# Last token tile of a decoder step: block loads and a VectorE transpose in place of TensorE transposes

## The reference, cut to what matters

```
hp = concatenate([meta, x_prompt], axis=1)      # 16 + 1024 rows of 1024
hs = x_sample                                   # 8 rows of 1024
# layer, for hp and hs alike
hn = rmsnorm(h, norm_mix)
z  = hn @ w_in                                  # 1024 -> 3584
u_in, c_gate, b_gate, q, k, v, g = split(z)
y_conv = b_gate * causal_conv3(c_gate * u_in)
o = retention(rotary(q), rotary(k) * QK_DIM**-0.5, v)   # 4 heads, chunks of 128
y_ret = head_rmsnorm(o) * silu(g)
h = h + concatenate([y_conv, y_ret]) @ w_out
h = h + square(relu(rmsnorm(h, norm_mlp) @ w_up)) @ w_down
```

## Time and profile before

| | us |
|---|---|
| median of 3 runs (1128.28 to 1129.99) | 1129.04 |
| the profiled execution | 1128.74 |
| its span | 1126.9 |
| PE busy | 1114.5 (99%) |
| VectorE busy | 784.3 (70%) |
| GpSimd busy | 551.5 (49%) |
| ScalarE busy | 418.1 (37%) |

### The profile page before, as it was taken

The page is one execution under the profiler, slowest core; times in us unless marked ns, Lnnn a source line. Parts: engine busy times, 40 slices in busy tenths (PEclk is TensorE's granted clock), DMA queues, the critical chain, the costliest instruction groups (busy, mean ns, idle before and its releaser), DMA issues.

```text
span 1126.9 us, 21879 instructions
## 1 busy us (share of the span) xinstructions
PE 1114.5 (99%) x8339; PEld 1096.2 (97%) x8339; DVE 784.3 (70%) x1171; ACT 418.1 (37%) x861; POOL 551.5 (49%) x535
## 2 busy tenths in 40 slices
PE   9999999999999999999999999999999999999996
PEld 7799999999999999999999999999999999999996
DVE  5455656566466766788777777777877776877856
ACT  6422313123124333543333333335552543444414
POOL 0154253252240611143322423223999899999992
PEclk9999999999999999999999999999999999999999
DMA  8951341422321231255344353438962544464314
GB/s 223 235 140 49 98 122 48 130 75 77 94 76 59 77 113 64 69 188 180 122 151 150 124 173 127 151 114 277 341 198 68 163 151 149 134 189 151 95 38 152
DMA packets 187482, 150.37 MB, mean 133 GB/s; under 512 B 32989, under 2 KB 149957, under 8 KB 187391
## 3 DMA queue, kind: packets, MB, share of 16 engines
q1 hardware_dynamic: 182295, 145.93, 41.4%
q10 hardware_dynamic: 5096, 3.20, 0.9%
HBM read 104.92 MB, written 44.20 MB: 132 GB/s over the span
## 4 chain that ended last, share of the span: by engine, by line
PE 98%; DMA 1%; SPq 1%; DVE 0%; issue 0%; DVEq 0%; ACT 0%
PE pair L2045 19%; PE pair L2046 19%; PE pair L2047 19%; PE pair L1832 8%; PE pair L1834 8%; PE pair L1833 8%; PE pair L2022 3%; PE pair L2024 3%; PE pair L2023 3%; PE pair L1890 1%; PE pair L1891 1%; PE pair L1893 1%; PE pair L1940 1%; PE pair L1943 1%; PE pair L1950 1%; PE pair L1939 1%
## 5 line engine op out<-in xcount | busy, mean ns | idle before, releaser
L2045 PE MATMUL pair<-m_hi,dn_hi 128*128 128x258 f32 (+2 forms) x896 | 254.7, 284 | 0.2 <-issue 0.2
L2046 PE MATMUL pair<-b_lo,up_hi 128*128 128x258 f32 x896 | 253.6, 283 | 0.0
L2045 PE MATMUL pair<-b_hi,up_hi 128*128 128x258 f32 x896 | 253.6, 283 | 0.0
L2046 PE MATMUL pair<-m_lo,dn_hi 128*128 128x258 f32 (+2 forms) x896 | 253.6, 283 | 0.0
L2047 PE MATMUL pair<-m_hi,dn_lo 128*128 128x258 f32 (+2 forms) x896 | 253.3, 283 | 0.0
L2047 PE MATMUL pair<-b_hi,up_lo 128*128 128x258 f32 x896 | 252.2, 282 | 0.0
L1832 PE MATMUL pair<-x_hi,w_both 128*128 128x344 f32 (+2 forms) x576 | 188.7, 328 | 0.1
L1834 PE MATMUL pair<-x_hi,w_both 128*128 128x344 f32 (+2 forms) x576 | 184.5, 320 | 0.0
L1833 PE MATMUL pair<-x_lo,w_both 128*128 128x344 f32 (+2 forms) x576 | 184.2, 320 | 0.0
L1800 DVE TENSOR_TENSOR hid<-pair,hid 128x516 f32<-128x516 f32 (+2 forms) x194 | 124.6, 642 | 75.1 <-PE pair L2047 72.1
L2045 PEld LDWEIGHTS pair<-b_hi,up_hi 128*128 128x128 f32 x896 | 169.3, 189 | 1.0 <-issue 0.8
(11 more groups left out here) (224 smaller groups left out, 2037.8 us busy)
## 6 DMA issues: line engine op xcount, KB each, us to landing
m_raw<-m_dram SPq DMA_DIRECT2D x56, 516.0 KB, 5.0
m_dram<-hid SPq DMA_DIRECT2D x64, 258.0 KB, 3.7
up_raw<-w_up_dram SPq DMA_DIRECT2D x32, 512.0 KB, 4.9
dn_raw<-w_down_dram SPq DMA_DIRECT2D x128, 128.0 KB, 2.4
w_raw<-w_in_dram SPq DMA_DIRECT2D x27, 512.0 KB, 3.7
m_dram<-hid SPq DMA_DIRECT2D x16, 774.0 KB, 3.8
h_dram<-hid SPq DMA_DIRECT2D x8, 516.0 KB, 3.1
h_in<-h_dram SPq DMA_DIRECT2D x16, 258.0 KB, 5.5
```

Of the source, the lines that this page charges most:

```text
L2045: m_.matmul(to, shs[k], mhs[k], start=STARTS[i] and k == 0, stop=False, skip_group_check=more)
L2046: m_.matmul(to, shs[k], mls[k], start=False, stop=False, skip_group_check=more)
```

## The change

Tile 8 is turned like tiles 2 to 7. `load_end_blocks` loads its rows a second time in runs of 32 floats into buffer 0 of `x_blk` with eight DMAs, four of 16 partitions (meta) and four of 8 (samples), once tile 6 has been turned out of that buffer. They stand on SyncE's queue behind tile 8's row loads and ahead of the tables. `x_turn(8)` waits for the eight loads and turns them into a new tile `x_last` with one transpose of 256 elements a partition. ScalarE's copies and VectorE's subtractions for tile 8 read `x_last` in place of PSUM and take all eight groups at once. PE's eight transposes of tile 8 go. The counts that later code waits for grow by one turn and eight loads.

```diff
-TURN0 = len(BLK)
-MOVED0 = 64 * len(BLK) // 2
+TURN0 = len(BLK) + 1
+MOVED_B = 64 * len(BLK) // 2
+MOVED_A = MOVED_B + 128
...
+        x_last = at("x_last", [KT, SQ], F32, o + XT * CH * 4 + 4 * KT * 56)
...
+            def load_end_blocks():
+
+                sp.wait_ge(turned, XT - 1 - BLK[2] + 1)
+                for src, r0, r1 in ((meta, 0, META), (xs.rearrange("b s d -> (b s) d"), META, LAST)):
+                    rows = src.rearrange("b (k q a) -> q b k a", q=4, a=SQ)
+                    for q in range(4):
+                        sp.dma_start(x_blk[0][SQ * q + r0:SQ * q + r1, :, 0, :], rows[q]).then_inc(sq_moved, 16)
...
+            load_end_blocks()
             sp.dma_start(cosr[:, :], io["cos_t"]).then_inc(tab_in, 16)
...
+                if i == XT - 1:
+                    act.wait_ge(turned, TURN0)
+                    s.activation(x_end[:, :, 0:LAST], x_last[:, :, 0:LAST], ACT.Copy)
+                    s.activation(x_end[:, :, LAST:32], x_last[:, :, 0:32 - LAST], ACT.Copy)
+                    for c0, c1, r0 in ENDS:
+                        ins = s.activation(x_hi[:, :, c0:c1], x_last[:, :, r0:r0 + c1 - c0], ACT.Copy)
+                    ins.then_inc(xhi_done, 2)
+                    return
...
+                if i == XT - 1:
+                    dve.wait_ge(xhi_done, 2 * i + 2)
+                    d.tensor_tensor(x_end[:, :, 32:32 + LAST], x_last[:, :, 0:LAST], x_end[:, :, 0:LAST], ALU.subtract).then_inc(pack_ready, 2)
+                    for c0, c1, r0 in ENDS:
+                        ins = d.tensor_tensor(x_lo[:, :, c0:c1], x_last[:, :, r0:r0 + c1 - c0], x_hi[:, :, c0:c1], ALU.subtract)
+                    ins.then_inc(xlo_done, 2)
+                    return
...
+                if i == XT - 1:
+                    dve.wait_ge(sq_moved, MOVED_A)
+                    d.transpose(x_last[:, :, :], x_blk[0][:, :, 0, :]).then_inc(turned, 1)
+                    return
...
-                if i + 1 in BLK:
+                if i + 1 in BLK or i + 1 == XT - 1:
                     x_turn(i + 1)
...
             for i in range(XT):
                 v_rows(i)
-                if i + 2 < XT and i + 2 not in BLK:
-                    transposes(i + 2)
```

More of the change, by code:

```diff
@@ L528, in turn_rest @@
             def turn_rest(h):
-                sp.wait_ge(sq_moved, MOVED0 + 176 * h + 16)
+                sp.wait_ge(sq_moved, MOVED_A + 176 * h + 16)
                 sp.dma_start(k_meta[0:META, :].rearrange("r (b s) -> r b s", s=SQ),
@@ L536, in turn_rest @@
                 sp.dma_start(kB_dram, kB_sq[:, :]).then_inc(kB_moved, 16)
-                sp.wait_ge(kB_moved, MOVED0 + 80 * h + 16)
+                sp.wait_ge(kB_moved, MOVED_B + 80 * h + 16)
                 for j in range(4):
@@ L544, in turn_o @@
                 sp.dma_start(o_dram, u_n[:, 0:CHUNKS * P]).then_inc(sq_moved, 16)
-                sp.wait_ge(sq_moved, MOVED0 + 176 * h + 112)
+                sp.wait_ge(sq_moved, MOVED_A + 176 * h + 112)
                 for j in range(4):
@@ L910, in x_high @@
                     return
-                for hf in halves:
[L912 to L921, removed]
+                if i == XT - 1:
[6 more added lines that the diff above has]
+                    return
+                for hf in halves:
+                    act.wait_ge(xT_done, 2 * i + hf + 1)
+                    src = XT_B[i % 2][hf][:, :].rearrange("p (k c) -> p k c", c=P)
+                    s.activation(x_hi[:, 4 * hf:4 * hf + 4, c0:c1], src, ACT.Copy).then_inc(xhi_done, 1)
             for i in range(XT):
@@ L976, in retention @@
                     if step < 0:
-                        wait_alone(act, sq_moved, MOVED0 + 176 * h + 96)
+                        wait_alone(act, sq_moved, MOVED_A + 176 * h + 96)
                         s.activation(k_meta[0:META, :], k_meta[0:META, :], ACT.Copy,
@@ L980, in retention @@
                     else:
-                        wait_alone(act, kB_moved, MOVED0 + 80 * h + 80)
+                        wait_alone(act, kB_moved, MOVED_B + 80 * h + 80)
                     s.activation(k_tok[:, c0:c0 + 4, :].rearrange("p c (b s) -> p b c s", s=SQ), src.rearrange("p (b c s) -> p b c s", b=4, s=SQ), ACT.Copy,
@@ L1312, in x_low @@
                     return
+                if i == XT - 1:
[5 more added lines that the diff above has]
+                    return
                 for hf in halves:
                     dve.wait_ge(xhi_done, 2 * i + hf + 1)
[L1315 to L1322, removed]
+                    src = XT_B[i % 2][hf][:, :].rearrange("p (k c) -> p k c", c=P)
+                    d.tensor_tensor(x_lo[:, 4 * hf:4 * hf + 4, c0:c1], src, x_hi[:, 4 * hf:4 * hf + 4, c0:c1], ALU.subtract).then_inc(xlo_done, 1)
             def x_turn(i):
+                if i == XT - 1:
+                    dve.wait_ge(sq_moved, MOVED_A)
+                    d.transpose(x_last[:, :, :], x_blk[0][:, :, 0, :]).then_inc(turned, 1)
+                    return
                 c0, c1 = tok(i)
@@ L1499, in head @@
                 if not last:
-                    wait_alone(dve, sq_moved, MOVED0 + 176 * h + 176)
+                    wait_alone(dve, sq_moved, MOVED_A + 176 * h + 176)
                     yr = y_raw[:, bass.ds(4 + h, 1), META:PROMPT].rearrange("p o (c b s) -> p (o c) b s", b=4, s=SQ)
```

## The result

The changed kernel takes 1133.3 us (median of 7 executions, 1129.6 to 1134.3) where the kernel before took 1129.37 on the same chip (7, 1127.81 to 1130.83): a ratio of 1.0031, 95% interval 1.0022 to 1.0040. It is slower, by 3.9 us; the prediction was 1128.2, in a range up to 1130.2. The execution that was profiled took 1129.6 with a span of 1127.8; it is the fastest of the seven (the spans of the others are 1130.0 to 1132.5).

A forecast was written before the change was run, and what follows sets the result against it. TensorE, busy 99% of the span and holding 98% of the chain, was taken to bound the kernel. Terms of -0.81 + 0 + 0 gave -0.8 us, from 1129.04 to 1128.2 us, range 1127.1 to 1130.2.

The forecast's parts named there:

- The transposes removed: PE between tiles 6 and 7: 0.61 us of transposes and 0.20 lost behind them go, 0.81 us gained.
- The last tile's operands: Tile 8's loads, turn and splits: ready between 51.2 and 54.5 us, before L1916's 55.72, so no cost.
- the rival that pays them in series: The eight transfers paid one after another, 20 us from 42.0: kernel 8.3 us slower, 1137.3; chance 2%.
- The loads behind the eight issues: SyncE's later loads are issued 3.4 us later; the first weight lands 2.5 later, hidden by 0.6 us.
- The price of an issue: SyncE's time for each of the eight loads: 0.43 us, 3.4 us in all.
- the rival's 5.8: SyncE's eight issues at the block loads' median, 0.69 and a gap of 0.04: 5.8 us.
- What of the delay reaches the landing: First input weight: of 3.4 us later issue, 2 to 2.8 reach its landing, 2.5 taken; a full queue swallows 1.6.
- What stands behind the landing: GpSimd's product, then ScalarE's `high` at 57.16: GpSimd may start up to 55.2, 3.1 us later at no cost.
- 59.61 forecast for head 0's start: First input projection matmul on PE moves from 60.42 to 59.61 us, if nothing else becomes late.
- the weights come late: First input weights land 4.2 to 7.0 us later through dearer issues: 1129.3 to 1132.1 us; chance 18%.
- `high` behind GpSimd: Sign of being wrong, ahead of the input projection: GpSimd's first gain ends behind 57.1 and ScalarE's `high` waits for it.
- a slack of 0.6 us: Margin by which the first weight's 2.5 us later landing was to stay hidden ahead of the input projection.

The follow-up runs named there:

- no loads: The changed kernel less its eight loads, the last tile turned out of stale rows: 1128.76 us, ratio 0.9996 to the kernel before.
- early loads: The changed kernel with an own buffer for tile 8's blocks, two loads ahead of the block loads of each of tiles 4 to 7: 1128.44 us, ratio 0.9997.
- the shapes' run: The kernel before with nine extra unread loads of several shapes, issued by SyncE at 52.7 us, where it is idle: one time of 1128.75 us.
- the second trace: The changed kernel run once more with no edit, to profile another execution: 1133.3 us, ratio 1.0035, span of the profiled execution 1130.3.
- The loads alone: The kernel before, PE's transposes kept, with the eight loads added and waited for on VectorE: 1132.64 us, ratio 1.0021.
- the weights held longer: The kernel before, without the eight loads, its first input weight's load held until ScalarE's copy of the row factors: 1136.24 us, ratio 1.0064.
- the weights ahead: The changed kernel with the first two input weights issued ahead of the tables: 1130.73 us, ratio 1.0015; run again for a second trace, 1131.93.
- the filler: The changed kernel with unread matmuls on PE between the last tile's product and head 0: 1139.22 us with 50, 1131.43 with 14.

## Why the prediction was wrong, step by step

**The transposes removed: right.** Tile 7 follows tile 6 with nothing between, in PE's timeline of the changed kernel:

```profile
50.17 0.40 PE L1911 MATMUL pair<-wv_lo,x_hi 128*128 128x512 f32 x1
50.41 0.39 PE L1907 MATMUL pair<-wv_hi,x_hi 128*128 128x512 f32 x1
50.63 0.39 PE L1908 MATMUL pair<-wv_hi,x_lo 128*128 128x512 f32 x1
```

The 0.24 from L1911 to the next replaces the 0.61 and 0.43 of the earlier trace rows. From tile 6's last matmul to the transpose of the row factors PE takes 5.83 us (50.17 to 56.00 in this view), where it took 6.61 (49.76 to 56.37): 0.78 less, of 0.81 predicted. With nothing late behind it, the spans of the profiled executions are 0.5 us (no loads) and 0.9 us (early loads) under before, on either side of that, though neither can be told from no change in the medians.

**The last tile's operands: right.** VectorE's turn and subtraction:

```profile
48.37 0.45 DVE L1341 STREAM_TRANSPOSE x_last<-x_blk 128x256 f32<-128x256 f32 x1 [1.31 <-DMA x_blk<-x_sample_dram]
...
49.81 0.36 DVE L1327 TENSOR_TENSOR x_end<-x_last,x_end 128x192 fp32r<-128x192 f32 x1 [0.99 <-ACT x_hi L927]
```

The eight had landed by 48.4 (48.0 to 51.7 expected), the turn took 0.45 (0.4), the operands were there by 50.5 and the last row factor by 51.55, well ahead of PE's 56. The loads overlapped; the rival that pays them in series fell. So did the Trainium skill's rule as it was weighed there ("DMA: Bandwidth & Descriptors", "Rules for kernel authors": coalesce many small transfers), in its mechanism: its verdict, slower, came true, but through the time that the issuing engine spends and not through the transfers.

**The loads behind the eight issues: this step failed**, in three of its terms. *The price of an issue.* I took 0.43 from k_meta's and kA_sq's rows, by partitions, length of run and number of descriptors. k_meta has four runs of 32 floats to a partition, the new loads eight; the shapes' run shows 0.44 for four and 0.62 to 0.70 for eight. The block loads, with 32 such runs, were on the page at 584 ns and more; I had used them only for the rival. Eight issues took 5.4 us in place of 3.4, nearly the rival's 5.8. *What of the delay reaches the landing.* I let a full queue swallow 1.6 us, as if the load would land in 3.7 in place of 5.3. In that stretch the DMA engines weren't full (share 0.64 in place of 0.99), and still the weight's load took 5.52 us and, in the second trace, 6.68. So of 5.08 us of later issue (45.77 to 50.85), 4.43 came out as later landing; in the second trace 5.59 of later issue came out as 6.1. Predicted: 2.5. *What stands behind the landing.* GpSimd's products of both weights now run at 56.5 to 60.26, the second beside `low`, which took 1.82 in place of 1.23. The sum of the first trace closes with these: 59.61 forecast for head 0's start, + (4.43 - 3.1) + (1.82 - 1.23) = 61.53; it is 61.48.

This is the rival *the weights come late*, to which I gave 18%, with its mark, `high` behind GpSimd. Its own time, 1129.3 to 1132.1, was still short of 1133.3: it counted the wait alone.

**What no step had: the clock.** The wait was priced at its length. The loads alone, the weights held longer and the second trace of the weights ahead show the granted clock at 0.50 for 3 to 6 us behind a wait of PE, worth 1.7, 3.0 and (3 x 0.5 + 0.11) 1.6 us. The Trainium skill has this, in "TensorE: Matmul & The Clock Gate", under "Why this matters for your kernels": avoid idle gaps between matmul bursts, or the clock goes back to its lower level; these three traces agree, while those with waits of 1.5, 1.6 and 3.7 us show no fall, so the length of the wait alone doesn't tell. Neither trace of the changed kernel itself shows it (waits of 1.5 and 3.7 us, the clock 1.00 behind both), so for its slower executions it is inferred, from the mean clocks and from the filler.

**Left open.** Which trait of a load sets the price of its issue; why the same load takes 5.52 us in one execution and 6.68 in another; and why the clock held behind a wait of 3.7 us and fell behind one of 2.2. The last two make this start differ from one execution to the next; how much of the changed kernel's spread they explain no run here shows.

No version beat the kernel before by more than can be measured: the early loads come to 0.9997 of it.

## What to carry to other kernels

A DMA off the critical path costs its issuing engine time, and that time is handed to every load behind it; take the price of an issue from a load as like it as can be, in partitions, runs and length of run, work the margin out with the dearest like row too, and follow the queue down to the first load that something waits for. A wait of TensorE can cost more than its length, so a slack of 0.6 us ahead of it isn't cover when the term above it is unsure by two. If small loads must be added, put them where the queue stands waiting anyway, with a buffer that lets them go early.

## What the runs showed of the hardware

- The time that SyncE spends on issuing one load from DRAM, in these traces: 0.57 to 0.62 us for 16 partitions x 8 runs of 32 floats, 0.61 for 32 x 8 x 32 and 0.67 to 0.76 for 8 x 8 x 32, the smallest and the dearest; 0.34 and 0.44 for 16 x 4 x 32, 0.43 for 16 x 1 x 128; 0.38 at the median for 128 x 8 x 128. The two shapes of the change cost the same in the crowded and in the calmer stretch, and 0.60 to 0.74 on ScalarE's queue.
- VectorE beside GpSimd. `low` has two inputs in SBUF, and so has GpSimd's product. Alone, `low` takes 1.23 us. When it starts in the middle of the second product it ends 1.08 us behind that product's end: 61.34 behind 60.26 in the changed kernel, 63.02 behind 61.93 in its second trace, 66.55 behind 65.47 with the weights held longer. With the weights ahead a subtraction of 0.36 us took 2.08:

```profile
51.63 1.90 POOL L760 TENSOR_TENSOR w_raw<-w_raw,prm 128x1024 f32<-128x1024 f32 x1 [51.19 <-DMA w_raw<-w_in_dram]
...
51.66 2.08 DVE L1336 TENSOR_TENSOR x_end<-x_last,x_end 128x192 fp32r<-128x192 f32 x1 [0.99 <-ACT x_hi L936]
```

  It started 0.03 us behind GpSimd and ended 0.21 behind GpSimd's end. The Trainium skill ("SBUF — State Buffer", "Who interferes with whom") says that a VectorE instruction with two inputs in SBUF contends with a GpSimd instruction that reads SBUF, and that the port pair they share is an exclusive lock; these rows agree.
- The granted clock fell to 0.50 (1.2 GHz) behind PE waits of 2.2, 2.3 and 5.6 us, for 3 to 6 us, and stayed at 1.00 behind waits of 1.5, 1.6 and 3.7.
